# Unread TensorE products at the stage borders and behind the first units of the prompt attention

## What is computed

```
q, k/v of three branches, gates, z_nsa, q_r, k_r, v_r, z_r = split(rms_norm(x) @ w_in)
compressed keys, values = silu(blocks of 32 rows @ w1) @ w2      (prompt, and 8 caches of 1024 rows)
o_nsa = gated sum of compressed, selected and sliding-window attention, T5 bias on every logit
o_ret = chunkwise retention, 8 heads, group norm
y = x + concat(o_nsa * silu(z_nsa), group_norm(o_ret) * silu(z_r)) @ w_out
outputs: y of prompt and sample, the new key and value rows, windows and retention states
```

## Time and profile before

| | us |
|---|---|
| three runs | 1018.35, 1019.42, 1020.18; median 1019.42 |
| the profiled execution | 1015.06 |
| its span, first to last instruction | 1013.4 |
| TensorE busy in the span | 933.8 (92%) |
| VectorE busy | 501.9 (50%) |
| ScalarE busy | 309.7 (31%) |
| GpSimd busy | 189.4 (19%) |
| mean granted TensorE clock | 0.968 |

### The profile page before, as it was taken

How to read it: one execution, slowest core, us unless ns; L and a number is a source line. 1 busy time by engine, 2 the same in 40 slices (tenths; PEclk the granted TensorE clock), 3 DMA queues, 4 the chain that set the end, 5 groups by cost and what they waited for, 6 DMA issues and landing times. The chain is left out here.

```text
span 1013.4 us, 15464 instructions
## 1 busy us (share of the span) xinstructions
PE 933.8 (92%) x5223; PEld 706.3 (70%) x5223; DVE 501.9 (50%) x1072; ACT 309.7 (31%) x692; POOL 189.4 (19%) x234
## 2 busy tenths in 40 slices
PE   5999999999999989999778898999999996789998
PEld 3676879997768787868568775566665654566785
DVE  4764244446144555450156356766675744464522
ACT  4311032223032324241010355645655642211100
POOL 1222213333002221100053102111011021452000
PEclk9999999999999999999989778999999997999999
DMA  7407520002520023113395410000000025778621
GB/s 256 143 6 177 138 84 1 2 1 73 213 94 6 1 83 104 53 38 107 91 205 144 115 31 22 22 21 22 1 22 22 1 81 187 204 218 276 200 85 46
DMA packets 91004, 91.11 MB, mean 90 GB/s; under 512 B 27629, under 2 KB 69661, under 8 KB 90565
## 3 DMA queue, kind: packets, MB, share of 16 engines
q1 hardware_dynamic: 70546, 71.66, 23.4%
q10 hardware_dynamic: 16700, 9.36, 3.5%
q0 software_dynamic: 3680, 9.10, 3.2%
HBM read 75.51 MB, written 23.49 MB: 98 GB/s over the span
## 5 line engine op out<-in xcount | busy, mean ns | idle before, releaser
L818 PE MATMUL ps<-w_high,x_high 128*128 128x512 f32 (+3 forms) x576 | 225.3, 391 | 4.6 <-DVE w_low L590 2.7
L820 PE MATMUL ps<-w_high,x_low 128*128 128x512 f32 (+3 forms) x576 | 220.6, 383 | 0.0
L819 PE MATMUL ps<-w_low,x_high 128*128 128x512 f32 (+3 forms) x576 | 220.3, 382 | 0.0
L818 PEld LDWEIGHTS ps<-w_high,x_high 128*128 128x128 f32 (+1 forms) x576 | 102.9, 179 | 37.2 <-issue 7.4
L820 PEld LDWEIGHTS ps<-w_high,x_low 128*128 128x128 f32 (+1 forms) x576 | 102.6, 178 | 28.0
L819 PEld LDWEIGHTS ps<-w_low,x_high 128*128 128x128 f32 (+1 forms) x576 | 102.9, 179 | 26.1
L1629 PE MATMUL ps<-k_high,q_stack 128*128 128x512 f32 (+3 forms) x192 | 77.9, 409 | 12.8 <-DVE a_stats L1514 12.5
L384 POOL TENSOR_TENSOR stats<-stats,small 128x8 f32<-128x8 f32 (+3 forms) x35 | 40.8, 1165 | 226.1 <-DVE stats L642 170.8
L1629 PEld LDWEIGHTS ps<-k_high,q_stack 128*128 128x128 f32 x192 | 38.8, 202 | 54.4 <-DVE a_stats L1514 28.6
L1671 PE MATMUL ps<-weights_turned,v_nat 128*64 128x512 f32 x264 | 72.5, 631 | 0.0
L1630 PE MATMUL ps<-k_low,q_stack 128*128 128x512 f32 (+3 forms) x192 | 67.0, 356 | 0.0
(11 more groups left out here) (311 smaller groups left out, 1526.6 us busy)
## 6 DMA issues: line engine op xcount, KB each, us to landing
w_raw<-in_w_in SPq DMA_DIRECT2D x48, 256.0 KB, 4.4
tmp_skew<-tmp_table SPq DMA_DIRECT2D x8, 576.0 KB
bias_full<-tmp_skew SPq DMA_DIRECT2D x8, 512.0 KB, 5.4
w_out_raw<-in_w_out SPq DMA_DIRECT2D x16, 256.0 KB, 5.0
y_rows_in<-tmp_y SPq DMA_DIRECT2D x8, 512.0 KB, 4.5
x_rows<-in_x_prompt SPq DMA_DIRECT2D x8, 512.0 KB, 5.6
out_y_prompt<-out_rows SPq DMA_DIRECT2D x8, 512.0 KB, 5.5
x_tile<-in_x_prompt SPq DMA_DIRECT2D x6, 512.0 KB, 3.8
```

The source lines that it names most:

```text
L818: nc.tensor.matmul(out, s.xh[:, k, rows], s.wh[:, k, 0:w], start=(k == 0), stop=False)
L819: nc.tensor.matmul(out, s.xh[:, k, rows], s.wl[:, k, 0:w], start=False, stop=False)
L820: ins = nc.tensor.matmul(out, s.xl[:, k, rows], s.wh[:, k, 0:w], start=False, stop=(k == KT - 1))
```

## The change

A helper `keep_clock` issues the same product a number of times into a place in PSUM that nothing reads afterwards, without a wait and without a semaphore. It is called at seven places of TensorE's program, 60 products in all. Nothing else is changed, and no other engine has an instruction more or less.

```diff
+def keep_clock(nc, out, stationary, moving, times):
+    for _ in range(times):
+        nc.tensor.matmul(out, stationary, moving, start=True, stop=True)
...
 project:
             pe.wait_ge(ident_ready, 2)
+            keep_clock(nc, s.ps[:, 0, 0:P], s.ident[:], s.ident[:], 15)
             pe.wait_ge(hot_in, 32)
...
             turn_x(0)
+            keep_clock(nc, s.ps[:, 0, 0:P], s.ident[:], s.ident[:], 6)
             for i in range(n_idx):
...
+            keep_clock(nc, s.ps[:, 4, :], s.xh[:, 0, 0:P], s.wh[:, 0, :], 10)
...
 compress:
             turn_keys()
             second(1)
+            keep_clock(nc, s.ps[:, 0, 0:2 * P], w1[:, 1, 0, :], kcs[:, 0, 0:2 * P], 3)
...
 attend_prompt:
                 if i < n_u:
                     score(i)
+                if i == 1:
+                    keep_clock(nc, s.ps[:, 1, :], s.qs[:, 0, 0:P], s.qs[:, 1, 0:512], 6)
...
                 done = upto
+            keep_clock(nc, s.ps[:, 1, :], s.qs[:, 0, 0:P], s.qs[:, 1, 0:512], 12)
...
 finish:
             turn_y(0)
             turn_y(1)
+            keep_clock(nc, s.ps[:, 0, 0:P], s.ident[:], s.ident[:], 8)
             proj(0, range(0, 4))
```

## The result

The changed kernel takes 1010.67 us, the median of 12 runs (1007.01 to 1017.11), beside 1018.34 us for the kernel before on the same chip (1015.85 to 1020.18). The ratio is 0.9933 with a 95% interval of 0.9913 to 0.9953: faster by 6.8 us, between 4.8 and 8.9.

The account below looks back on a forecast made before the run. TensorE, busy 92% of the span, was taken as the bound, with half-rate stretches at borders. Terms -0.8 + 0.1 + 0.1 - 0.3 - 2.0 = -2.9 us, taken from the 1019.42 median, gave 1016.5; range 1013.6 to 1019.6.

Parts of the forecast that it names:

- The start: Projection start: six products behind turn_x(0) raise the clock, turn_x(1) moves from 22.62 to 21.77; 0.8 us gained.
- The last stage: Opening behind the attention: the clock holds, key transposes come 2.55 us earlier; taken as 2.0 gained.
- The cut from 2.55 to 2.0 for the key load: Last stage: some gain can be lost at the key load, with DMA engines over their full share; 2.0 taken.
- I take the same difference from it: Whole kernel: the 2.9 us computed on the profiled execution is taken off the 1019.42 median, giving 1016.5.
- The borders: Ten products ending the projection and three ending the compression buy nothing and cost 0.1 us each.
- The six in the attention: Behind the second attention unit: first unit at full, clock falling within or just behind it; 0.3 us gained.
- The clock holds through the attention: Rival, first attention units: full rate kept, 4 us beyond the forecast, 1012.5; chance 0.10.
- Swallowed: Rival: key load timing and x_tile pacing swallow the start and last-stage gains, leaving 1019.3; chance 0.18.
- Transposes do not count: Rival, last stage: the clock falls while y is transposed, the stage gives 0, 1018.5; chance 0.10.
- The rule quoted in the prediction: Transposes do not bring TensorE to full rate; by it the last-stage part would be worth nothing instead of 2.0.
- Slower: Rival, behind borders: unread products run at half and stand in the way, +3.4 us, 1022.8; chance 0.10.

Follow-up runs that it names:

- control: The kernel before, unchanged, run again to see how far its own executions lie apart; 1017.75 us, ratio 1.0001.
- control_2: The kernel before, unchanged, run once more for a third profile of its start; 1021.35 us in one execution.
- att_only: The change cut to the three products ending the compression and the six behind the second attention unit; 1018.67 us, ratio 0.9982 to the kernel before.
- eight_only: The change cut to the eight products between the transposes of y and the first product with w_out; 1017.74 us, ratio 1.0007 to the kernel before.
- twelve_only: The change cut to the twelve products at the end of the attention; 1017.36 us, ratio 0.9996 to the kernel before.
- finish_only: The change cut to the twelve products ending the attention and the eight behind the transposes of y; 1015.0 us, ratio 0.9941 to the kernel before.
- start_only: The change cut to the fifteen and the six products at the start of the projection; 1014.33 us, ratio 0.9960 to the kernel before.
- no_finish: The change without the twelve products at the end of the attention and the eight in the last stage; 1015.58 us, ratio 0.9972 to the kernel before.
- no_att6: The change without the six products behind the second attention unit; 1010.67 us, ratio 0.9926 to the kernel before.
- no_b10: The change without the ten products at the end of the projection; 1010.74 us, ratio 0.9940 to the kernel before.
- hold: The change plus 21 unread products of 512 columns behind early attention units; 1006.51 us, ratio 0.9879 to the kernel before.
- hold_q: The change plus 21 products in the attention and twelve in the projection's wait for the last query rows; 1004.96 us, ratio 0.9875 to the kernel before.

## Why the prediction was wrong in size

The fourteen profiles, each one execution, by six stretches that follow each other without a gap (us; starts of TensorE's rows): A, from the start to the last transposes of x; P, from there to the end of the projection's products; B, from there to the first attention unit; N, from there to the transposes of y; C, from the transposes of y to the second of the key transposes (behind 24 products with `w_out`); D, from there to the end of TensorE's work.

| kernel | added products at | A | P | B | N | C | D |
|---|---|---|---|---|---|---|---|
| before | none | 71.02 | 426.1 | 74.19 | 278.8 | 17.08 | 143.2 |
| control | none | 71.14 | 426.2 | 74.41 | 276.3 | 18.05 | 145.7 |
| control_2 | none | 73.39 | 426.4 | 72.71 | 277.3 | 19.93 | 147.0 |
| att_only | 3, 6 | 73.81 | 427.7 | 75.63 | 277.1 | 17.99 | 145.5 |
| eight_only | 8 | 71.29 | 426.3 | 73.45 | 279.1 | 17.83 | 142.4 |
| twelve_only | 12 | 73.17 | 427.7 | 73.93 | 277.7 | 19.77 | 142.8 |
| finish_only | 12, 8 | 72.36 | 426.5 | 73.71 | 277.7 | 15.51 | 145.1 |
| start_only | 15, 6 | 70.05 | 427.0 | 73.15 | 277.8 | 17.26 | 143.3 |
| no_finish | all but 12, 8 | 70.04 | 427.9 | 74.98 | 276.9 | 18.04 | 142.1 |
| no_att6 | all but 6 | 70.18 | 427.2 | 75.31 | 276.2 | 15.52 | 143.3 |
| no_b10 | all but 10 | 70.19 | 426.7 | 74.26 | 276.8 | 15.49 | 142.2 |
| change | all | 69.77 | 426.1 | 74.45 | 276.9 | 14.57 | 142.8 |
| hold | all and 21 | 70.25 | 425.9 | 74.42 | 271.3 | 14.52 | 147.7 |
| hold_q | all and 33 | 70.36 | 424.3 | 75.07 | 269.8 | 15.54 | 145.4 |

*The start: right mechanism, term too small.* The prediction took -0.8, from 22.62 to 21.77, and that is what the pair of profiles shows (5.53 to 4.75 us). But in column A the seven starts without the products lie between 71.0 and 73.8, mean 72.3, and the seven with them between 69.8 and 70.4, mean 70.1. The products are worth 2.2 us, and nothing of it is given back by the end of the projection (column P has a mean of 426.7 without them and 426.8 with them, `hold_q` left out). The profile that the forecast read was the quickest of the seven.

*The last stage: right mechanism, term too small.* Computed 2.55, taken 2.0. Column C without the pair of the twelve and the eight is 17.1 to 19.9 (mean of six 18.1; of the kernels with one of the two, 17.8 and 19.8); with both it is 14.5 to 15.5, mean 15.2: 2.9 us. Again the profile of before had the shortest of its kind. Of the six with both, the clock stays at full through C in two (change and `hold`, 14.5) and falls with the second eight transposes, as in `finish_only`, in the four others (15.5); the full opening of the changed kernel's profile is in part luck. The cut from 2.55 to 2.0 for the key load has no support: column D is 144.5 in the mean without both and 144.4 with them, so no loss is seen there.

*The step that failed* is the size of two terms of the sum, -0.8 for the start (2.2 measured) and -2.0 for the last stage (2.9 measured), and behind both "I take the same difference from it": the terms were read as losses of one quick execution, and then taken off a median that was 4.4 us above it. Of the 96 other executions of the unchanged kernel that were timed, three are quicker than 1015.06; the mean granted clock, 0.968 in that profile, is 0.962 over the 83 of `control` and of the unchanged kernel beside the experiments. Part of those 4.4 us were the same half-rate stretches, longer, and the change takes them away too. The honest term was a mean loss, for which one profile gives only one draw. Of the miss of 5.8 us, 1.1 are the base (the median of three runs was 1019.42, that of the twelve beside the change 1018.34), and 4.8 the gain.

Not every draw was a quick one. The pair of profiles differs by 5.9 us, and its largest surplus over the forecast lies in column N: 1.9 us shorter, where 0.3 was forecast. There the profile of before was slow, the second longest of the eight without the six (276.2 to 279.1, mean 277.6; the four with them, `hold` and `hold_q` left out, have 276.9).

*The borders.* Forecast +0.2 for the ten and the three. Column B has a mean of 73.9 without the ten and 74.9 with them, spread over 2.9 and 0.9; from the last product of the projection to the first transposes it is 4.2 instead of 4.0. A cost between 0.2 and 0.9 us, and no gain, as said.

*The six in the attention.* Forecast -0.3 with the clock falling again. In the changed kernel the second compressed unit begins 0.7 us sooner against the first; over all profiles without `hold`'s products that distance is 15.3 without the six and 15.1 with them, and column N is 0.7 us shorter. Right in size; but the gain is not made at the third unit, where VectorE waits for the six, and it comes with the units behind it, which run at full up to 579.

*The rivals.* "The clock holds through the attention" did not happen: 0.50 from 580 to 590. It was priced at 4 us in all and put at 0.10 on the ground that VectorE and ScalarE take turns with TensorE; `hold` shows that the price was there to be had (5.6 us in its attention). "Swallowed" falls with column D and a key load of 6.91 us. "Transposes do not count" falls with the sixteen transposes at 507.30, behind which, with no other product near, the clock went from half to 1.00 within 510 to 511. The rule quoted in the prediction from the Trainium skill ("TensorE: Matmul & The Clock Gate", Part 4: PE-mode transpose) does not agree with this trace. The opening at full would not show it alone, since in four other profiles the clock fell while y was transposed. "Slower" falls: the clock was at full at 570.35 and 847.20. Its mechanism is there in small, in the 1.50 us that VectorE waits for the six, and in `eight_only`: eight products behind a lost clock, 0.5 us in the way.

*What stays open.* The columns make -2.2 (A) + 0.1 (P) + 0.9 (B) - 0.7 (N) - 2.9 (C) + 0.0 (D) = -4.8, and the ratio says -6.8, at least -4.8. They meet only at the edge of the interval; `start_only` and `finish_only`, too, gain more in their medians (4.1 and 6) than columns A and C show (2.2 and 2.9). The six columns leave out none of TensorE's time, so what is missing is not another stretch. Three profiled executions of before (1015.06, 1016.51, 1021.35) against three of the change or nearly it (change, no_att6 and no_b10: 1009.20, 1012.23, 1010.35) differ by 7.0 us in their means; 2.5 us of that lie in column D, where the time follows none of the added products (no_finish has the shortest, `hold` the longest). It goes with the mean granted clock of that stretch instead: 0.99 in the four profiles with 142.1 to 143.2 us, 0.98 in the eight with 142.4 to 145.7, 0.97 in the two with 147.0 and 147.7. Draws of the clock of that size are the likeliest cause of the difference; it is not shown, nor whether the clock lengthens the stretch or a longer wait lowers the clock.

## What to carry to other kernels

When a loss depends on where a clock falls, one profile is one draw: take several of the unchanged kernel, price the loss by their mean, and don't carry a sum made against a quick execution over to the median. Fill every wait of a border or none: here twelve products alone and eight alone gave nothing, together some 4 to 6 us. An engine that looks busy at half rate can be the bound although its neighbours seem to take turns with it; here 21 unread products of 0.23 us, 4.9 us of TensorE's time, left the kernel some 4 us faster.

## What the runs showed of the hardware that was not expected

The same program loses the clock at different points in different executions: behind the same wait of 1.2 us for `x_tile` it fell in control_2 and not in control. Unread products of 512 columns among products of 32 and 128 columns took the granted clock from 0.50 to 1.00 from 580 to 590 us (`hold`) while TensorE was busy for less of the time (9.08 instead of 9.76 of 10 us). And how far a raised clock reached differed from place to place: the 15 at the start were followed by a table at full rate and, behind a wait of 2.42 us, by transposes at half; the twelve of `twelve_only` held it across a wait of 1.42 us and lost it behind the next one, of 1.07 us.
